# Stage buffers at multiples of 256 bytes, and 528 columns taken as 272 and 256 side by side in PSUM

## What is computed

```
h = concat([meta, x])                                   # 528 tokens
h = h + concat([mlstm(...), forgetting_attention(...)]) @ w_out     # from rmsnorm(h) @ w_in
h = h[:, 16:]
h = h + peer(rmsnorm(h))        # top-16 product keys, 16384 experts, u and v tables of 64 MB each

h = concat([meta_2, h])
h = h + 0.5 * rmsnorm(swiglu(rmsnorm(h), ffn1_wi, ffn1_wo))         # D_FF = 2816
h = h + rmsnorm(hybrid_mixer(rmsnorm(h)))               # Fourier, short convolution, gated delta
h = h + 0.5 * rmsnorm(swiglu(rmsnorm(h), ffn2_wi, ffn2_wo))
out = h[:, 16:]
```

## The kernel before

| stage | tiles x blocks x 3 parts | products |
|---|---|---|
| first block's projections (`hn1`) | 25 x 8 x 3, every token; 4 x 8 x 3 kept | 600 pairs of 264; 96 of 512 |
| out projection (`y1`) | 8 x 8 x 3 | 192 of 512 |
| queries (`hn2`, L311) | 16 x 8 x 3 | 384 of 512 |
| experts (`hn2` at L514, `units` at L543) | 256 x 8 x 3 | 6144 of 384 |
| first feed-forward (`f1_hn`, `f1_g`) | 44 x 8 x 3 and 8 x 22 x 3 | 1584 pairs of 264 |
| mixer (`hn3`, `br0`, `br1`) | 29 x 8 x 3 every token; 28 x 8 x 3 and 16 x 4 x 3 kept | 696 pairs of 264; 864 of 512 |
| mixer's end (`br2`, `m`) | 8 x 4 x 3 and 8 x 8 x 3 | 288 of 512 |
| second feed-forward (`f2_hn`, `f2_g`) | as the first, kept | 1584 of 512 |

## Time and profile before

### The profile page before, as it was taken

One profiled execution on the slowest core, in us unless ns is written; L12 is line 12 of the kernel. 1 busy time (PEld: TensorE's weight loads), 2 busy tenths in 40 slices (PEclk: granted clock), 3 DMA queues, 4 the chain that ended last, 5 costly groups with the idle time before them and its releaser, 6 DMA issues. The chain is left out here.

```text
span 3177.0 us, 50383 instructions
## 1 busy us (share of the span) xinstructions
PE 3122.1 (98%) x19569; PEld 2879.1 (91%) x19569; DVE 1953.3 (61%) x3576; ACT 1242.5 (39%) x1892; POOL 624.3 (20%) x468
## 2 busy tenths in 40 slices
PE   8999999999999999999999999999999999999999
PEld 8976789999999999999999999998897899778887
DVE  7344489988888768888875333354454565554333
ACT  4234423457777533333334212232233333343232
POOL 0010205863333324333310001101000000201011
PEclk9999999999999999999999999999999999999999
DMA  4210224689999999999962323222222000223232
GB/s 154 80 40 1 80 75 143 203 289 342 334 338 342 356 331 348 357 361 356 354 220 93 110 77 98 64 91 98 87 80 70 5 1 1 93 73 118 76 103 68
DMA packets 160148, 517.03 MB, mean 163 GB/s; under 512 B 18928, under 2 KB 51824, under 8 KB 156656
## 3 DMA queue, kind: packets, MB, share of 16 engines
q1 hardware_dynamic: 75632, 279.93, 25.8%
q0 software_dynamic: 44032, 159.40, 14.5%
q10 hardware_dynamic: 40320, 75.52, 6.4%
HBM read 462.35 MB, written 52.43 MB: 162 GB/s over the span
## 5 line engine op out<-in xcount | busy, mean ns | idle before, releaser
L185 DVE TENSOR_TENSOR w_lo<-ring,w_hi 128x1024 fp32r<-128x1024 f32 (+2 forms) x157 | 205.9, 1312 | 549.5 <-ACT w_hi L179 549.5
L179 ACT ACTIVATE w_hi<-ring 128x1024 fp32r<-128x1024 f32 (+2 forms) x170 | 190.0, 1118 | 435.6 <-PE ps L245 362.1
L245 PE MATMUL ps<-f_hn_hi,w_hi 128*128 128x264 f32 (+1 forms) x1056 | 279.3, 319 | 0.8 <-DVE w_lo L185 0.7
L245 PE MATMUL ps<-f_hn_hi,w_lo 128*128 128x264 f32 (+1 forms) x1056 | 278.5, 318 | 0.0
L245 PE MATMUL ps<-f_hn_lo,w_hi 128*128 128x264 f32 (+1 forms) x1056 | 278.5, 318 | 0.0
L486 ACT ACTIVATE w_hi<-ring 128x1024 fp32r<-128x1024 f32 x170 | 180.0, 1059 | 224.0 <-PE ps L543 220.8
L490 DVE TENSOR_TENSOR w_lo<-ring,w_hi 128x1024 fp32r<-128x1024 f32 x144 | 176.4, 1225 | 111.5 <-ACT w_hi L486 111.4
L514 PE MATMUL ps<-hn_hi,w_hi 128*128 128x384 f32 x680 | 231.4, 340 | 2.4 <-POOL w_lo L490 2.4
L543 PE MATMUL ps<-units_hi,w_hi 128*128 128x384 f32 x680 | 227.2, 334 | 2.1 <-DVE units_lo L868 2.1
L514 PE MATMUL ps<-hn_lo,w_hi 128*128 128x384 f32 x680 | 227.3, 334 | 0.0
L514 PE MATMUL ps<-hn_hi,w_lo 128*128 128x384 f32 x680 | 227.3, 334 | 0.0
(11 more groups left out here) (476 smaller groups left out, 8140.4 us busy)
## 6 DMA issues: line engine op xcount, KB each, us to landing
ring<-in_w_uv SPq DMA_DIRECT2D x256, 512.0 KB, 6.1
ring<-in_f_up SPq DMA_DIRECT2D x88, 512.0 KB, 3.4
expert_units<-scratch ACTq DMA_DIRECT2D x128, 192.0 KB, 5.0
gate_table<-peer ACTq DMA_DIRECT2D x24, 1024.0 KB, 8.2
peer<-gate_table POOLq DMA_DIRECT2D x64, 384.0 KB, 8.8
peer<-expert_units ACTq DMA_DIRECT2D x128, 192.0 KB, 5.9
ring<-in_w_in SPq DMA_DIRECT2D x29, 512.0 KB, 3.5
ring<-in_w_late SPq DMA_DIRECT2D x25, 512.0 KB, 3.4
```

What stands on the lines that cost most here:

```text
L179: self.nc.scalar.activation(self.h[:, self.slot(k), 0:self.cols], e.ring[:, self.ring(k), 0:self.cols], ACT.Copy).then_inc(e.hi_done, 1)
L185: self.nc.vector.tensor_tensor(self.l[:, self.slot(k), 0:self.cols], e.ring[:, self.ring(k), 0:self.cols], self.h[:, self.slot(k), 0:self. ...
L245: mm = nc.tensor.matmul(e.ps[:, bank + hf, 0:tokens.width], lhsT[:, wt.slot(k), col], rhs(part, c)[:, cut], start=(c == 0 and j == 0), sto ...
```

## The change

Nothing that is computed changes, and no product, instruction of another engine or wait is added. Three things do:

1. **Addresses.** A filler buffer `edge` moves the stage buffers to a multiple of 256 bytes (87552 = 342 x 256). `hn1`, `f1_hn` and `f1_g` get the lead of `LEAD` = 48 columns (192 bytes) that `hn3` had, so that column 16, where the kept tokens begin, stands on a multiple of 256. To have that for `g` too, `hn` and `g` of a feed-forward lie in one region, with `y` behind it. Now every kept operand and all weights start at 0, rows of `hn1`, `hn3`, `f1_hn`, `f1_g` at 192.
2. **The cut.** 528 columns are taken as 272 (starting at 192 and ending on a multiple of 256) and 256 (starting at 0), instead of 264 and 264.
3. **PSUM.** The 272 results go to the last 272 columns of one bank, the 256 to the first of the next, side by side over the edge; DVE reads them as one flat row of 528 (`Tokens.tile` on `e.psf`). The sums over channels of `Front` and `Close` keep the halves.

```diff
@@ Tokens
-        self.own_parts = [(0, self.own)] if kept else self.parts
+        self.pieces = [(0, slice(0, T), self.cols)]
+        self.own_pieces = [(0, slice(0, T), self.own)]
+        if not kept:
+            self.pieces = self.own_pieces = [(0, slice(WIDE - PART, WIDE), slice(0, PART)),
+                                             (1, slice(0, L - PART), slice(PART, L))]
...
+    def tile(self, e, bank):
+        at = bank * WIDE + WIDE - PART
+        return e.ps[:, bank, :] if self.kept else e.psf[:, at:at + L]
@@ tile_matmuls
-            for hf, cut in tokens.own_parts if own else tokens.parts:
-                mm = nc.tensor.matmul(e.ps[:, bank + hf, 0:tokens.width], lhsT[:, wt.slot(k), col],
+            for at, to, cut in tokens.own_pieces if own else tokens.pieces:
+                mm = nc.tensor.matmul(e.ps[:, bank + at, to], lhsT[:, wt.slot(k), col],
@@ Ffn.dve (Mixer and the first block's stage alike)
-            z, p = tk.banks(e, 2 * (k % SLOTS)), it * 2 + (self.pairs[s] + k // 2 + 1)
+            z, p = tk.tile(e, 2 * (k % SLOTS)), it * 2 + (self.pairs[s] + k // 2 + 1)
@@ hybrid_kernel
+        at = -(-nc.sbuf_base // 32) * 32
+        sb("edge", -at % EDGE // 4)
         with ExitStack() as outer:
-            shared = Region(nc, outer, "columns1", 2 * 4 * DC * ROW)
-            hn = [shared.at(f"hn1_{x}", i * 4 * DC * ROW, DC, ROW, dt=F32R) for i, x in enumerate(("hi", "lo"))]
+            shared = Region(nc, outer, "columns1", 4 * (LINE + 2 * DC * ROW))
+            hn = [shared.at(f"hn1_{x}", 4 * (LEAD + i * DC * ROW), DC, ROW, dt=F32R) for i, x in enumerate(("hi", "lo"))]
@@ ffn
-                hn = [sb(f"{name}_hn_{x}", DC, own, dt=F32R) for x in ("hi", "lo")]
+                rows = Region(nc, inner, f"{name}_rows", 4 * (LINE + 2 * (DC + FSPLIT) * own))
+                hn = [rows.at(f"{name}_hn_{x}", 4 * (lead + i * DC * own), DC, own, dt=F32R)
+                      for i, x in enumerate(("hi", "lo"))]
+                g = [rows.at(f"{name}_g{x}", 4 * (lead + (2 * DC + i * FSPLIT) * own), FSPLIT, own, dt=F32R)
+                     for i, x in enumerate(("hi", "lo"))]
```

More of the change, by code:

```diff
@@ L45 @@
 ROW = 9 * LINE
+EDGE = 4 * LINE
+LEAD = LINE - META
+PART = META + EDGE
 def const_tables():
@@ L1231, in dve @@
         self.front.dve_scale(dve)
-        r = tk.view(e.r1)
+        r = e.r1[:, self.cut]
         def tile(s, it, k):
@@ L1238, in tile @@
             self.w[s].computed(dve, it, k)
-            z, p = tk.banks(e, 2 * (k % SLOTS)), it * 2 + (self.pairs[s] + k // 2 + 1)
+            z, p = tk.tile(e, 2 * (k % SLOTS)), it * 2 + (self.pairs[s] + k // 2 + 1)
             if s % 2 == 0:
-                x, y = (tk.view(v[:, k // 2 % 2]) for v in (self.act_of, self.prod))
+                x, y = (v[:, k // 2 % 2, self.cut] for v in (self.act_of, self.prod))
                 if k % 2 == 0:
@@ L1250, in tile @@
             elif s == 1:
-                V.tensor_copy(tk.view(self.y[:, k]), z).then_inc(self.taken, 1)
+                V.tensor_copy(self.y[:, k, self.cut], z).then_inc(self.taken, 1)
             else:
-                y = tk.view(self.y[:, k])
+                y = self.y[:, k, self.cut]
                 V.tensor_tensor(y, y, z, ALU.add).then_inc(self.taken, 1)
@@ L1649, in evac @@
             if n < self.N_MIX:
-                V.tensor_tensor(halves(b.z2[:, n]), EVERY.banks(e, z), halves(r), ALU.mult).then_inc(self.taken, 1)
+                V.tensor_tensor(b.z2[:, n], EVERY.tile(e, z), r, ALU.mult).then_inc(self.taken, 1)
             elif n < self.QKV:
@@ L1662, in evac @@
             elif n < self.GATE:
-                V.tensor_tensor(halves(b.z3[:, n - self.QKV]), EVERY.banks(e, z), halves(r),
-                                ALU.mult).then_inc(self.taken, 1)
+                V.tensor_tensor(b.z3[:, n - self.QKV], EVERY.tile(e, z), r, ALU.mult).then_inc(self.taken, 1)
             elif n == self.GATE:
                 dve.wait_ge(self.silu, self.N_QKV)
-                V.tensor_tensor(halves(b.g.raw), e.ps[0:16, z:z + 2, 0:HL], halves(r[0:16]),
-                                ALU.mult).then_inc(self.taken, 1)
+                V.tensor_tensor(b.g.raw, EVERY.tile(e, z)[0:16], r[0:16], ALU.mult).then_inc(self.taken, 1)
             else:
@@ L1908, in evac @@
             if n == 0:
-                V.tensor_tensor(halves(g.raw), e.ps[0:16, z:z + 2, 0:HL], halves(r[0:16]),
-                                ALU.mult).then_inc(self.taken, 1)
+                V.tensor_tensor(g.raw, EVERY.tile(e, z)[0:16], r[0:16], ALU.mult).then_inc(self.taken, 1)
                 return
@@ L1924, in evac @@
                 o = self.z[:, n - 1]
-            V.tensor_tensor(halves(o), EVERY.banks(e, z), halves(r), ALU.mult).then_inc(self.taken, 1)
+            V.tensor_tensor(o, EVERY.tile(e, z), r, ALU.mult).then_inc(self.taken, 1)
         def conv(k):
@@ L3015, in ffn @@
                 sb = space(inner)
-                own = T if tokens.kept else ROW
-                hn = [sb(f"{name}_hn_{x}", DC, own, dt=F32R) for x in ("hi", "lo")]
+                own, lead = (T, 0) if tokens.kept else (ROW, LEAD)
+                rows = Region(nc, inner, f"{name}_rows", 4 * (LINE + 2 * (DC + FSPLIT) * own))
[3 more added lines that the diff above has]
+                     for i, x in enumerate(("hi", "lo"))]
                 y = sb(f"{name}_y", DC, L)
-                g = [sb(f"{name}_g{x}", FSPLIT, own, dt=F32R) for x in ("hi", "lo")]
                 w = parts(inner, 2, SLOT)
@@ L3029, in hybrid_kernel @@
             half_slot = 4 * 2 * SLOT
-            pad, rows = 4 * (LINE - META), 4 * DC * ROW
+            pad, rows = 4 * LEAD, 4 * DC * ROW
             front = Region(nc, outer, "mix_front", 2 * half_slot + 4 * LINE + 2 * rows)
```

## The result

The changed kernel takes 3188.9 us (median of 6 runs, 3187.25 to 3190.64), the kernel before 3176.78 beside it (6 runs, 3173.62 to 3181.19): a ratio of 1.0038, 95% interval 1.0026 to 1.0050. It is slower by 12 us where I forecast 109 us faster. 3189 lies outside my range, beyond rival 3 (3179), and in its direction it is rival 4, at a third of that rival's price. Executions of the kernel before lie partly near 3172 us, at a mean granted clock of 0.998 to 0.999, and partly near 3180, at 0.995 to 0.996, so its median moves between 3176 and 3180 with the share of each.

A forecast was written before the change was run, and what follows sets the result against it. PE was taken to bound the kernel, with DMA close behind in the experts. Gains of 36 us (512 columns), 28.8 (pairs) and 44 (384 columns) made 108.8 off 3177.0; with 2.1 to the median, 3070 us, range 3030 to 3110.

The forecast's parts named there:

- rival 3: All products: time goes by columns by 32, rounded down, plus one, whatever the start; nothing gained, 3179 us, chance 0.09.
- rival 4: Pairs: start at byte 192 costs a whole 256-byte line, 253.3 ns a pair, 38 us lost, 3217 us; chance 0.05.
- Time by blocks touched: All float32r products: time follows 128-byte blocks touched, 13.33 ns each; a start on a block's edge spares one.
- 36 us (512 columns): Products of 512 columns from byte 0: 215.0 ns, 11.7 less each over 3408 products, less about 4 us: 36 us gained.
- 44 us (384): Expert products of 384 columns: 161.7 ns, 11.6 less each; 71.5 us if PE stayed alone, 44 us gained beside DMA.
- DMA's ceiling: Expert stage: DMA share can rise to 1.03, leaving room for 7% in the first half, 4% in the second.
- the waits: Expert stage: PE waits now and then for POOL, and for gates from HBM at the turn; 2 us off for each.
- the three corrections of that part: Expert stage: 2 us off for POOL in tiles 0 to 43, 2 at the turn between halves, 2 for bursts.
- The row from byte 96: Products of 512 columns from byte 96 took 229.0 ns, 2.3 more than from byte 32, so the start counts.
- Plain float32 as the floor: Plain float32 products, 264 columns as two passes of 111.7 ns, gave the floor: columns' time and 1.7 ns.
- Pairs: Products of 272 and 256 columns: 230.0 ns a pair, 10.0 less, over 2880 pairs 28.8 us gained; bounds 24 and 38.
- At nothing: DVE's flat read over the bank's edge, the filler and the new place of `y` were priced at no time.

The follow-up runs named there:

- lengths: Separate small kernel without the computation: 48 bare products per cell over many lengths and starts; 512 columns take 226.6 ns from byte 0, 233.3 from byte 32.
- halves_flat: Changed kernel with 264 and 264 columns instead of 272 and 256, still side by side over the bank edge and read flat: 3172.85 us, ratio 0.9995.
- halves_aligned: Changed kernel with the cut back at 264 and 264 at the starts of two banks, read as two pieces, new addresses kept: 3179.45 us, ratio 1.0001.

## Why the prediction was wrong

**Time by blocks touched: the step that failed.** I had three distances (120.0, 173.3, 226.7) that fitted "blocks of 128 bytes touched", the long ones from byte 32 only. I read a cause into a coincidence: 9, 13 and 17 blocks were columns plus one block of 13.3, as rival 3 put it, and no row had 512 columns from a block's edge to tell them apart. I saw that (the text of rival 3 says so) and still gave it 0.09. Rival 3's rule isn't right either: it has 272 columns at 120.0 ns, and they take 125.4. Of the sum, 36 us (512 columns) and 44 us (384) are 0. DMA's ceiling, the waits and the three corrections of that part never came into play, since PE didn't get faster; in the experts' second half the DMA share is 0.96 at 352 GB/s, with as many products in the same 420 us.

**The row from byte 96.** I took its 2.3 ns as evidence that the start counts, and so against rival 3. It does count, but against the weights' start: there it was 64 bytes behind, which the bare products give as 228.9. The long products had row and weights at the same start almost everywhere before, and the change kept that, so what a start gives 384 and 512 columns was had already. The Trainium skill, page "SBUF — State Buffer", section "Who interferes with whom", gives PE a read port of its own for the moving operand and another for weights, independent of each other. This case doesn't bear that out: 226.9 against 233.3 ns by 32 bytes between the two starts are not two reads that leave each other alone.

**Plain float32 as the floor.** I read the counts of these rows as products, and they are records, two a product (48 products leave 96 in `lengths`). So 264 columns take 446.7 ns, four times 111.7 and not two, and products of 4 columns come 223 ns apart. The 1.7 ns came from that slower type; the floor of 111.7 is right for float32r all the same, which is luck. bfloat16 shows 2.5 over its columns, float32r at 256 columns and more never under 6.6 (113.3 at 256, from byte 192). The Trainium skill, page "TensorE: Matmul & The Clock Gate", section "Wait — 56ns, not 53.3ns?", gives N / 2.4 + 2.5 ns from product to product at the upper clock. bfloat16 here agrees to 0.1 ns (215.8 at 512), float32r with a weight load for each product doesn't (226.7).

**Pairs: wrong sign.** I had -10.0 ns and my bounds went from -8.3 to -13.3; it is +6.5 in the feed-forward, and the term of 28.8 us gained became some 16.6 lost. 256 columns take 120.0, not 110, when they start where the weights do: my bound of 120.0 for nine blocks stood only in rival 4. And 272 take 125.4, which none of my cases had. I should have bounded the pair from above by its columns and the 13.3 that 384 and 512 show: 2 x 13.3 + 220.0 = 246.7. That was in the earlier trace rows.

**Rival 4** had the right deciding point, a pair past 240.0 with the long products unchanged, and the wrong mechanism: not byte 192 (256 first from there costs nothing), and 6.5 ns rather than 13.3. That it had the sign right is luck. **At nothing** held: the flat read, the filler, the place of `y` cost nothing, by halves_flat.

**From pairs to the median.** 600 x 4.1 + 1056 x 6.5 + 528 x 6.7 + 696 x 5.4 are 16.6 us. Without the clock, the stage table has 9.9 us of it in the first feed-forward, where 10.4 belong, 3.0 in the mixer of 3.8, and 0.9 in the first block of 2.5. Against it stand the 3.4 us of the clock, and 1.3 in the experts that I can't place. The nearest kernel to set beside is `halves_aligned`, with pairs of 240.0 ns at the same addresses: its way is 17.1 us shorter, 1.7 of that by the clock (10.2 us at the lower level, not 13.7), so 15.4 are left for the cut. Beside the kernel before at 3172 us the changed kernel is the whole 16 to 17 us slower as well.

**What stays open.** Why a float32r product with its weight load takes mostly 10 to 13 ns over the columns, and up to 20, with the same weights or others, and why 32 weight columns cost as much as 128; by what rule cut, start and history give a pair 240 ns or anything up to 250; and why the lower clock comes more often in one kernel than in another. The runs show that reading the row is the limit and that the two starts count against each other. A picture of how the two reads take turns would be a guess.

## What to carry to other kernels

A rule that fits three numbers and whose rival fits them too is not a rule: find the one row that would differ, or price the plan by the rival. Before a sum of 80 us is hung on "the start of a row", a bare stretch of 48 such products from each of two starts settles it in 11 us each. With float32r and a weight load for each product, count some 13 ns over the columns and, for 384 and 512 columns, keep row and weights at the same start within 256 bytes; a short piece can be quicker elsewhere (256 columns take 113.3 ns at 192 bytes apart, 120.0 at none). After any recut of a pair, read the distance of two pairs again, since the order of the same two pieces was worth 16 us here.

## What the runs showed of the hardware

- float32r products, each with its own weight load, are never closer than 111.7 ns in the mean (16, 192 and 224 columns), and take 7 to 20 ns over their columns from 256 columns on, mostly 10 to 13; bfloat16 takes 2.5.
- The start of the row against that of the weights: equal 226.7 to 226.9 ns at all eight starts for 512 columns, 64 bytes apart 228.9, 32 apart 233.3 to 233.4. For 256 columns it is the other way round: equal 120.0, 192 apart 113.3.
- Every second element of a float32r row: 230.0 ns for 256 columns, against 120.0, and 232.9 at the lower clock.
- The same weights loaded again cost as much as others: 226.7 ns for 512 columns.
- Plain float32 leaves two records a product, each of its columns twice and 2.5 ns: 215.8 ns at 256 columns, so 431.6 a product.
- At the lower clock the overhead of a dense float32r row is gone: 264 columns in 220 ns, 272 in 226.7, 384 in 320.
- A pair of 272 and 256 columns from byte 192 can hold either of two levels, 242.2 or 246.7 ns, by what ran ahead of it.
- With products of 64 of the 128 rows the granted clock fell to 0.50, and PE was busy for 8.00 of 8 us there.
